# GpSimd adds the scaled tiles into x in the post norms of block 1

## What is computed

```python
def hybrid_layer(x, g_mix_pre, g_mix_post, g_mlp_pre, g_mlp_post, w_in, rel_bias,
                 conv_w, conv_b, conv_ln_g, conv_ln_b, w_out, w_up, w_down):
    h = rms_norm(x, g_mix_pre)
    u = h @ w_in
    ...
    mix = jnp.concatenate([y_att, y_conv, y_ret], axis=-1) @ w_out
    x = x + rms_norm(mix, g_mix_post)
    h = rms_norm(x, g_mlp_pre)
    f = jnp.square(jax.nn.relu(h @ w_up)) @ w_down
    return x + rms_norm(f, g_mlp_post)
```

## Time and profile before

| | |
|---|---|
| median of 3 runs | 3647.18 us (3645.04 to 3649.38) |
| profiled execution | 3640.97 us |
| its span | 3639.2 us |
| busy: PE, DVE, ACT, POOL | 3449.4, 1647.0, 1232.2, 207.0 us |
| block 1, layer 0: first post norm | from 324.55 us |
| block 1, layer 0: second post norm | from 694.82 us |
| block 1, layer 1: first post norm | from 1008.94 us |
| block 1, layer 1: second post norm | from 1376.99 us |

### The profile page before, as it was taken

How to read it: one execution, slowest core, us unless ns; L and a number is a source line. 1 busy time by engine, 2 the same in 40 slices (tenths; PEclk the granted TensorE clock), 3 DMA queues, 4 the chain that set the end, 5 groups by cost and what they waited for, 6 DMA issues and landing times.

```text
span 3639.2 us, 45622 instructions
## 1 busy us (share of the span) xinstructions
PE 3449.4 (95%) x15812; PEld 2665.4 (73%) x15812; DVE 1647.0 (45%) x2137; ACT 1232.2 (34%) x1827; POOL 207.0 (6%) x247
## 2 busy tenths in 40 slices
PE   7989999898899998999999999999999999999998
PEld 5647888575678886888665678887888776578886
DVE  3755443556454335443345553434443444654333
ACT  3333122432431224322344432323232344442323
POOL 1200000012010000000001310000000001200000
PEclk9999999999999999999999999999999999999999
DMA  5213322231233222332321033332332221023331
GB/s 155 64 35 71 97 92 98 65 92 47 64 85 96 94 88 84 93 97 93 75 64 30 21 91 98 93 97 82 98 93 98 76 64 46 13 78 97 97 92 64
DMA packets 416615, 289.24 MB, mean 79 GB/s; under 512 B 23520, under 2 KB 394380, under 8 KB 416216
## 3 DMA queue, kind: packets, MB, share of 16 engines
q1 hardware_dynamic: 413592, 280.74, 26.5%
q0 software_dynamic: 2736, 4.58, 0.8%
q10 hardware_dynamic: 144, 2.10, 0.2%
HBM read 285.25 MB, written 2.13 MB: 79 GB/s over the span
## 4 chain that ended last, share of the span: by engine, by line
PE 88%; DVE 5%; issue 3%; ACT 3%; DVEq 0%; DMA 0%; ACTq 0%; SPq 0%
PE bank L1657 26%; PE bank L1659 26%; PE bank L1658 26%; PE bank L1667 2%; PE bank L1744 1%; PE bank L1790 1%; PE bank L1766 1%; PE bank L1836 1%; PE bank L1870 1%; DVE hl L1235 0%; PE bank L2060 0%; PE bank L2058 0%; PE bank L1697 0%; DVE stat L1307 0%; PE bank L2049 0%
## 5 line engine op out<-in xcount | busy, mean ns | idle before, releaser
L1657 PE MATMUL bank<-hh,whi 128*128 128x512 f32 x2896 | 1165.4, 402 | 55.6 <-DVE hl L1235 26.2
L1658 PE MATMUL bank<-hl,whi 128*128 128x512 f32 x2896 | 1138.7, 393 | 0.0
L1659 PE MATMUL bank<-hh,wlo 128*128 128x512 f32 x2896 | 1137.7, 393 | 0.0
L1218 DVE TENSOR_TENSOR wlo<-raw,whi 128x1024 fp32r<-128x1024 f32 (+2 forms) x536 | 644.8, 1204 | 437.4 <-ACT whi L860 422.9
L1657 PEld LDWEIGHTS bank<-hh,whi 128*128 128x128 f32 x2896 | 551.6, 190 | 213.9 <-DVE hl L1235 41.6
L1658 PEld LDWEIGHTS bank<-hl,whi 128*128 128x128 f32 x2896 | 552.0, 191 | 117.0 <-issue 7.1
L1659 PEld LDWEIGHTS bank<-hh,wlo 128*128 128x128 f32 x2896 | 550.6, 190 | 117.6
L860 ACT ACTIVATE whi<-raw 128x1024 fp32r<-128x1024 f32 (+2 forms) x536 | 547.7, 1033 | 249.7 <-PE bank L1659 249.1
L1657 PE MATMUL bank<-fshi,whi 128*128 128x512 f32 (+2 forms) x1316 | 517.7, 393 | 14.4 <-DVE fslo L1483 14.1
L1658 PE MATMUL bank<-fslo,whi 128*128 128x512 f32 (+2 forms) x1316 | 506.9, 385 | 0.0
L1659 PE MATMUL bank<-fshi,wlo 128*128 128x512 f32 (+2 forms) x1316 | 506.8, 385 | 0.0
(11 more groups left out here) (219 smaller groups left out, 2377.8 us busy)
## 6 DMA issues: line engine op xcount, KB each, us to landing
raw<-in_ffn_w_gate SPq DMA_DIRECT2D x88, 512.0 KB, 3.8
raw<-in_ffn_w_up SPq DMA_DIRECT2D x88, 512.0 KB, 3.8
raw<-in_ffn_w_down SPq DMA_DIRECT2D x88, 512.0 KB, 3.4
raw<-in_w_in SPq DMA_DIRECT2D x82, 512.0 KB, 3.9
raw<-in_w_up SPq DMA_DIRECT2D x64, 512.0 KB, 4.1
raw<-in_w_down SPq DMA_DIRECT2D x64, 512.0 KB, 3.3
raw<-in_w_out SPq DMA_DIRECT2D x16, 512.0 KB, 3.9
raw<-in_w_in SPq DMA_DIRECT2D x16, 256.0 KB, 3.3
```

The costliest lines, as they stand in the source:

```text
L1218: dve.tensor_tensor(slot3(wlo, s, m), slot3(raw, s, m), slot3(whi, s, m).bitcast(F32), ALU.subtract).then_inc(c.lo_done.sem, 1)
L1657: pe.matmul(o, wh, ah, start=start, stop=False)
L1658: pe.matmul(o, wh, al, start=False, stop=False)
L1659: return pe.matmul(o, wl, ah, start=False, stop=stop)
```

## The change

POOL gets 16 additions per layer at the end of its layer's program. Each waits until DVE has written a scaled tile (the new count scaled_y), adds it into x and counts x_ready, as DVE's add did. DVE's post_norm keeps the scalings and gained_low. Scaling t still waits for the add of tile t - 2, whose tmp it overwrites. DVE_STEPS is the number of steps that DVE's own count states for a layer: 16 fewer.

```diff
-ACT_STEPS, DVE_STEPS = (2, 16), (95, 48)
+ACT_STEPS, DVE_STEPS = (2, 16), (79, 48)
...
+            c.scaled_y = signal("scaled_y", 2 * KT, 0)
...
                         tables(2)
+                for k in range(2 * KT):
+                    t = k % KT
+                    pool.wait_ge(c.scaled_y.sem, c.scaled_y.at(l, k + 1))
+                    pool.tensor_tensor(x[:, t, :], x[:, t, :], tmp[t % 2], ALU.add).then_inc(c.x_ready.sem, 1)
             c = counts_of(1)
...
             def post_norm(c, l, r, x0, gains, behind=None):
 
-                def add(t, ahead):
-                    dve.wait_ge(c.dve_step.sem, c.dve_step.at(l, c.dve_step.k - ahead))
-                    dve.tensor_tensor(x[:, t, :], x[:, t, :], tmp[t % 2], ALU.add).then_inc(c.x_ready.sem, 1)
                 dve.wait_ge(c.rn_rstd.sem, c.rn_rstd.at(l, r))
                 for t in range(KT):
                     y = g(F_AT) if t == 0 else bank[:, t, :]
                     if t >= 2:
                         dve.wait_ge(c.x_ready.sem, c.x_ready.at(l, x0 + t - 1))
-                    dve.scalar_tensor_tensor(out=tmp[t % 2], in0=y, scalar=gains[:, t:t + 1], in1=rstd, op0=ALU.mult, op1=ALU.mult).then_inc(c.dve_step.next(), 1)
-                    if t:
-                        add(t - 1, 1)
+                    dve.scalar_tensor_tensor(out=tmp[t % 2], in0=y, scalar=gains[:, t:t + 1], in1=rstd, op0=ALU.mult, op1=ALU.mult).then_inc(c.scaled_y.sem, 1)
                     if behind and t > 1:
                         behind(t - 2)
-                add(KT - 1, 0)
                 if behind:
                     behind(KT - 2)
                     behind(KT - 1)
```

## The result

| kernel | median (us) | runs | ratio to before, 95% interval |
|---|---|---|---|
| before | 3648.93 (3645.04 to 3651.49) | 6 | |
| changed | 3669.19 (3665.87 to 3671.89) | 6 | 1.0055 (1.0042 to 1.0068) |

The change costs 20.3 us, 15 to 25 by the interval; forecast were 23.6 us and a time of 3670.8. That the time is off by only 1.6 us is in part luck: the change is 3.3 us smaller than forecast, and the six runs of before have a median 1.75 us above that of the three known at the forecast. The profiled execution of the changed kernel took 3666.43 us, with a span of 3664.6.

What follows compares the result with a forecast made beforehand. The kernel was taken as bound by TensorE's matmul stream (88% of the span). Second post norms -0.9, first +0.5, layer 1's loads +9.1, block 2's +13.9, clock +1.0: +23.6 us on 3647.18 gives 3670.8 us, range 3661 to 3687.

Steps and rivals of the forecast that it cites:

- end of the second post norm's last add: After the down product: scaling, hand-over and eight POOL adds take 10.45 us against 10.92, ending 0.47 us earlier, twice.
- each of the first post norms, net: After the output product: adds contend with DVE's low-part subtraction, partly hidden by TensorE's slack; +0.25 us each, +0.5 in all.
- last add to first issue: End of a layer: POOL issues the first waiting load 0.30 us after the last add.
- layer 1: first issue to last landing: Layer 1's eight parameter loads, now behind layer 0's adds, take 16.1 us until the second conv_w load lands.
- layer 1, net of the adds' gain: Layer 1's opening norm waits for the late loads: +9.1 us, less the 0.47 gained by the adds.
- block 2: first issue to last landing: Block 2's table and twelve parameter loads, now behind layer 1's adds, take 16.5 us to land.
- block 2, net, first scaled copy: ACT's first scaled copy in block 2 waits for late gains: +13.9 us, less the 0.47 gained by the adds.
- clock of block 2's first unit: After 16 us of idleness TensorE restarts at half clock in block 2's first unit; +1.0 us (0.5 to 2).
- mechanism: Layer 1's and block 2's loads queue behind POOL's adds, delaying DVE's norm and ACT's first copy: +9.1 and +13.9 us.
- quick adds: Second rival: POOL adds take 0.76 us in all post norms and the load sets land quickly; 3662.9 us, chance 0.11.
- dear adds: First rival: POOL adds take 1.93 us, so both kinds of post norm end later; 3684.8 us, chance 0.14.
- third rival: POOL's parameter loads do not come late and cost nothing; 3646.8 us, or 3640.4 with adds of 0.76 us; chance 0.05.

Runs made afterwards that it cites:

- e4: Changed kernel, but DVE's low-part subtraction in the norm behind the first post norm reads its second input from PSUM instead of SBUF; one run, 3667.83 us.
- e3: Kernel before, all adds on DVE, but POOL holds layer 1's and block 2's loads back until the post norms' last add; 3672.11 us, ratio 1.0065.
- e2: Changed kernel, but only layer 1's parameter loads are issued between the adds; block 2's table and loads stay behind them; 3662.83 us, ratio 1.0040.
- e5: Changed kernel, but the two conv_w loads stand first instead of last among layer 1's eight late loads; 3668.57 us, ratio 1.0047.
- e1: Changed kernel, but POOL issues layer 1's loads and block 2's table and loads between the first and second post norms' adds; 3649.13 us, ratio 1.0002.
- e6: Changed kernel with all loads issued between the adds, except layer 1's three norm gains, which stay behind the 16 adds; 3649.18 us, ratio 1.0005.
- e7: Changed kernel with all loads issued between the adds, except block 2's 1 MB table, which stays behind layer 1's adds; 3651.94 us, ratio 1.0012.

## Why the prediction was right, step by step

| step | forecast | shown by the changed kernel |
|---|---|---|
| an add of POOL, second post norm | 1.2 us | 9.86 / 8 = 1.23 |
| end of the second post norm's last add | -0.47 | 10.69 for 10.92: -0.23 |
| an add of POOL, first post norm | up to 1.87 | 12.65 / 8 = 1.58, and 1.70 beside low parts |
| end of a first post norm's last add (14.27 before) | up to 15.8 | 13.48 |
| each of the first post norms, net | +0.25 | none that can be seen |
| last add to first issue | 0.30 | -0.06 |
| layer 1: first issue to last landing | 16.1 | 713.88 + 7.93 - 707.31 = 14.5 (15.2 in e4, 15.6 in e3) |
| layer 1, net of the adds' gain | +8.6 | +6.9 (25.25 - 18.36) |
| block 2: first issue to last landing | 16.5 | 1406.50 + 5.86 - 1396.52 = 15.8 |
| block 2, net, first scaled copy | +13.4 | +12.6 (26.49 - 13.93) |
| clock of block 2's first unit | +1.0 | +1.5 (1.3 by the third unit), and 0.2 to 0.3 in e2, e4, e5 |
| sum | +23.6 | +20.3 in the medians |

**The mechanism** was right in both places: the loads behind the adds in POOL's queue, the norm that opens layer 1 forecast near 722 and at 721.93, ACT's first scaled copy forecast near 1413 and at 1412.38, each released by the very load that was named. That the first of these times fits to the tenth is luck: in this trace the second post norm's first scaling came 1.86 us later than in before, which makes up for a pause 1.7 us shorter than forecast (8.6 - 6.9). e3 shows that late loads are enough, e1 that nothing else above its noise is in it, e2 that block 2's place costs 14.7 of the 20.3 us alone, e5 that the last landing ends the pause.

**What was mis-sized** is mostly layer 1's set, 1.6 us of it in this trace. I priced the landing of the second conv_w load between the median of its kind and its maximum, 9.3 to 9.9 us; it was 7.9. The rows of before came from loads that were issued in the middle of the up product, or at the program's start; now TensorE and DVE pause beside them. The pause alone is not the reason, for they pause in e4 and e3 too, whose chains have:

```profile
711.07 8.65 DMA prm<-in_conv_w
```
```profile
715.92 9.00 DMA prm<-in_conv_w
```

The landing of one and the same load scatters from 7.9 to 9.0 us in these three traces, so about 1 us of this term is the luck of the execution, and the forecast stood above all three. And I took the hand-over of 0.30 us from the earlier trace rows, where POOL waited for DVE. Now the last add stands in POOL's own queue, and the load's issue is shown to begin 0.06 us before the add's end: no hand-over shows within the engine. That is some 0.35 us in each of the two places. The chain after the change lists them one behind the other:

```profile
700.00 7.37 POOL x L816 x6
707.37 0.90 POOL prm L790
...
713.88 7.93 DMA prm<-in_conv_w
721.80 0.03 issue
```

**The second post norms** gained 0.23 us each at the last add, and this goes nowhere. Where the loads are early the norm of layer 1 starts at 18.91 (e1), 18.30 (e6) and 19.19 (e7) against 18.36 before. Between the last square and the table load of ACT that follows stands a wait that the profile puts down to nothing, 1.94 us before, 2.73 in e1, 2.08 in e6:

```profile
708.42 1.28 ACT L1044 ACT_TABLE_LOAD   x1 [1.94 <-issue]
```
```profile
711.09 1.28 ACT L1064 ACT_TABLE_LOAD   x1 [2.73 <-issue]
```
```profile
710.06 1.28 ACT L1068 ACT_TABLE_LOAD   x1 [2.08 <-issue]
```

The first row is of before, then e1, then e6. It varies by more than the adds give; what makes it vary stays open. The rival "quick adds", with A = 0.76, is out; so is "dear adds", at 1.93, since the adds took 1.23.

**The first post norms** I had put at +0.25 each, out of a last add that would end up to 1.5 us later. The last mean matmul of PE in the two of them, timeline of the changed kernel:

```profile
343.75 1.02 PE L1666 MATMUL bank<-G,c_sb 128*128 128x512 f32 x2
```
```profile
1032.49 1.02 PE L1666 MATMUL bank<-G,c_sb 128*128 128x512 f32 x2
```

From the first scalings at 327.67 and 1015.66 that is 16.08 and 16.83 us. Before it was 341.35 - 324.55 = 16.80 and 1025.02 - 1008.94 = 16.08: the same two values, the other way round. In the seven other traces it is 15.98 to 17.00, with DVE's adds (e3: 16.08 and 16.83) and with the undisturbed adds of e4 (16.83 and 16.81) alike. TensorE paces this place, as the earlier trace rows had it, whatever the adds take.

The 15.8 us of the prediction failed in one step besides: it charged all eight adds with a low part beside them. The first two have hardly any, and the last add ended (0.83 + 12.65) = 13.48 us after the first scaling, 0.8 us earlier than with DVE's adds and not 1.5 later. The contention was real, its price nothing; the sum should have had 0 there.

**The third rival**, that the loads do not come late, had its deciding point at a landing 7.4 us after the last add. e6 stands on the near side of it (5.3 us: no cost), the changed kernel on the far side (14.4 us: +6.9). The two agree with the bound, though they leave everything between 5.3 and 14.4 us open.

**The clock** was the one term with a spread of its own. All runs with a long pause ahead of block 2 restart at half clock:

```profile
1414.00:1418.00 4.00, 4.00 (x10) 3.13 (x11) 4.00 (x7) 3.97 (x8) 0.00 (x0) 0.50 0.00 0
```

(the changed kernel; busy time of PE, PEld, DVE, ACT, POOL, then the granted clock, 0.50 being 1.2 GHz). In this trace the clock stays at 0.50 until 1420, 6 us after TensorE's restart at 1413.94. In e5, with the same program from layer 1's norm on, TensorE restarts at 1412.23 and has full speed again for most of the stretch from 1415:

```profile
1415.00:1418.00 3.00, 3.00 (x13) 2.49 (x12) 1.91 (x4) 2.95 (x6) 0.00 (x0) 0.89 0.02 5
```

From the first scaled copy to the second unit it is 8.50 us before, 10.00 in the changed kernel and 9.99 in e3, but 8.68, 8.77 and 8.73 in e2, e4 and e5, whose pause is as long. So the term was 0.2 to 1.5 us, in three traces below the 0.5 us that the prediction had as its lower end. The changed kernel and e5 have the same program in this stretch and stand at either end, so the program there does not decide it alone; with one trace of each, what does is not shown.

## What to carry to other kernels

When instructions are given to an engine whose queue also issues loads, list first what stands behind them in that queue, and for each of those find when its consumer needs it: the moved work costs what its neighbours in the queue lose, here 20 us for 32 adds that are themselves free. The cure is an order, not a speed: the same loads issued between two groups of the adds cost nothing (e1). And for the consumer's side follow the waits through the in-order queue and not only the operands: in e7 a table that no early matmul reads held up the first matmul, because the engine that makes its operand waits for the table first.

## What the hardware showed that was not expected

**Both sides of the SBUF contention stretch.** Beside DVE's low part (two SBUF inputs) POOL's add took 1.70 us instead of 1.23, and the low part 1.10 instead of 0.73; e4 removes one of the low part's SBUF inputs and both are back (1.25 and 0.73). The Trainium skill (SBUF — State Buffer, "SBUF: two separate sides") says that the shared port pair is held for a whole instruction by the one that starts first while the other fully blocks. That the pair is shared, and by which forms, the traces bear out: DVE's scaling, with one input in PSUM, keeps its 0.74 beside the same adds. Whether it is held for a whole instruction they leave open. Had add and low part, one each per tile, kept each other out for all of the time that they show, a tile would need 1.23 + 0.73 = 1.96 us, and it took 1.70. But if 0.34 us of an add needs no port (an estimate: the fixed part that the prediction worked out from the earlier trace rows), it would be 1.62, and 1.70 lies between.

**The granted clock fell in a place where it had not before.** In the kernel before, TensorE waited 2.91 us ahead of block 2 and ran its first unit at full speed. In e1 it waited 3.16 us, with the same work around it; it restarted at full speed (0.50 us for the first matmul, as in the earlier trace rows) and fell to half about a microsecond later. Window rows of e1, with the granted clock before the last two columns:

```profile
1396.00:1398.00 2.00, 2.00 (x7) 1.57 (x7) 2.00 (x4) 2.00 (x4) 0.00 (x0) 0.62 0.86 247
1398.00:1400.00 2.00, 2.00 (x6) 1.52 (x6) 1.81 (x3) 1.97 (x4) 0.00 (x0) 0.52 0.03 7
```

The second unit comes 22.99 us after the first scaling instead of 22.43, 0.56 us later, although the copy is 0.23 us earlier; e6 shows the same (22.96). From the third unit on it is 0.4 us in both (28.43 and 28.40 instead of 28.05). So the 0.23 us that POOL's adds save at the end of layer 1 were, in these two executions, more than given back. Whether the longer wait or the place in time is what tipped it was not tried.
